# Layer ends, layer starts and gates of a four-block network, reordered on one core

## The chip, the cores and the metric

The kernel runs on one core of a Trainium2 chip. The metric is the device time of one execution in microseconds (us). A core has TensorE (PE, matrix products), VectorE (DVE), ScalarE (ACT), GpSimd (POOL) and SyncE (SP, which here only issues transfers). PEld is TensorE's loading of its stationary operand, PEclk the clock granted to it as a share of full speed. Each engine works through its own instructions in order and meets the others at semaphores.

## The reference

The input x has 256 rows (tokens) of 1024 numbers, all in fp32. Two "first" blocks come first, then a final norm, then two "second" layers of an attention and a feed-forward part each. Cut to what the change touches:

```python
# first block, layer 0 and 1
h = rms_norm(x, norm_w[layer])
(q, k, v, z_attn, q_h, f_h, i_h, g_h, gate_attn, gate_hgrn) = split(h @ w_in[layer])
a = sliding_window_attention(q, k, v, sinks) * silu(z_attn)
o = hgrn2_recurrence(silu(q_h), kin, i_h, logf)       # decays exp(G_t - G_s)
b = rms(o) * hgrn_norm_w * silu(g_h)
merged = sigmoid(gate_attn) * (a @ w_up_attn) + sigmoid(gate_hgrn) * (b @ w_up_hgrn)
x = x + merged @ w_out

# second block, i = 0 and 1; mod comes from silu(c) @ ada_w + ada_b
h = x * (1 + sc_t) + sh_t
y = dsa_mixer(h) if i == 0 else diff_mixer(h)         # each ends in o @ w_o
x = layer_norm(ALPHA * x + (1 + g_t) * y, ln_g[i, 0], ln_b[i, 0])
h = x * (1 + sc_c) + sh_c
y = square(relu(h @ w1)) @ w2                         # 1024 -> 4096 -> 1024
x = layer_norm(ALPHA * x + (1 + g_c) * y, ln_g[i, 1], ln_b[i, 1])
```

## The kernel before

The tokens are two tiles of 128 rows. The stages follow each other: f0 and f1 (the first blocks), s0 (the selecting attention), s1 (feed-forward), s2 (the differential attention) and s3 (feed-forward).

Every product is done in three matmuls, since each fp32 operand is split into a high and a low part: high x high, low x high, high x low (`product_tok`, lines 340 to 342, token-major output, 512 columns at a time; `product_feat`, lines 347 to 349, feature-major output, 256 columns). Weights come in units of 4 k blocks by 512 columns, in halves of 512 KB: SP loads a half into `ring` (line 873), ScalarE casts it to `whi` (line 1037), POOL subtracts that to get `wlo` (line 928), TensorE multiplies. A ring of four units and three slots (PARTS = 3) of `whi`/`wlo` tie these four together. Two more kinds of weights pass through the same ring: the ada_w slabs (line 492), whose products give the modulation of the second layers, and the pieces of s0's latent projection (sixteen small transfers).

What each engine does and when is written out as a program for each. On ScalarE, `ahead(name, more)` casts the weight halves up to three (PARTS) plus `more` beyond those of `name` before the next operation goes; POOL has `lows` for the same. PSUM has eight banks of 512 columns: two turns of two banks for projections (`lin_ps`) and two for everything else (`tmp_ps`). `open_lin` and `open_tmp` on TensorE take the next turn and wait until its last reader has released it.

In the first blocks, the recurrence runs over levels: ScalarE evacuates one projection per level (line 1186: i, z, g, ga0), exps the gate sums (line 1177), VectorE forms factors (lines 1576, 1577) and gathers (line 1586), TensorE multiplies (line 594). Then the attention follows in four groups: scores (line 506), maximum (line 1434), exps (line 1082), transposes (line 402), their copies (line 1097), products (line 529). Between these TensorE runs projections gh0 and gh1; `gate` on ScalarE (line 1199) evacuates ga1, gh0 and gh1 with a sigmoid in the same operation. ACT_TABLE_LOAD stands where ScalarE changes its function table. Then come the transposes bT and aT of the two branches, split by lines 1062 (high) and 1357, 1358 (low), and the products uh0, uh1, ua0, ua1 with `w_up`.

At the end of a layer, `last_by_tiles` runs the last k units of both column halves y0, y1 so that tile 0 is complete first. VectorE's `residual` adds (lines 1759, 1760), takes statistics (lines 1766 to 1768) and, behind POOL's power (line 946), normalises (line 1744; in s3 lines 1750, 1751, which give the result). At the start of the next stage, `turned_by_tiles` transposes x (line 425) into two tmp turns, `keep_busy` (line 408) puts filler matmuls ahead of them (BUSY gives how many), and `mixed` applies the modulation while it splits: ScalarE high (line 1227), VectorE low in pairs of blocks (lines 1716, 1719) and the release of the turn (line 1724). In the feed-forward parts VectorE also scales and shifts x (`affine`, lines 1781, 1784) behind this, and squares the hidden activation (line 1796), which ScalarE casts (line 1257) and VectorE splits (line 1798).

## Time and profile before

| | us |
|---|---|
| median of 3 runs | 1180.23 (1179.15 to 1180.48) |
| profiled execution | 1184.73 |
| its span | 1183.0 |
| PE busy | 1082.4 |
| POOL busy | 772.2 |
| ACT busy | 550.7 |
| DVE busy | 518.8 |

The span is the profiler's stretch from first to last instruction; the profiled execution's own time is 1.7 us more. Busy times of matmuls overlap their neighbours' (they are pipelined), so a stretch of matmuls is best read from the distance of their starts. In a timeline's row, what stands in brackets is the idle time of the engine before it and the instruction that ended it; "DVEq" is VectorE's queue, here the nop at line 1724 that releases a turn. "x8" says that eight such instructions stand in a row.

### The profile page before, as it was taken

The numbers are of one execution on the slowest core, as the hardware profiler recorded it, in microseconds if no ns is written. First come the engines' busy times: TensorE is split into PE (matmuls) and PEld (weight loads), VectorE is DVE, ScalarE is ACT, GpSimd is POOL, SyncE is SP. The second block draws the span as 40 slices with busy tenths as digits, with TensorE's granted clock in tenths as the row PEclk, the third lists the DMA queues.
The fourth block names the chain that finished last, engine by engine and source line by source line (L and its number), as shares of the span: only waits on it lengthen the run. The fifth ranks groups of instructions, "written<-read, shape, count | busy, mean of one in ns | idle before, by whom it ended". The sixth has DMA issues, their size and how long they took to land.

```text
span 1183.0 us, 16461 instructions
## 1 busy us (share of the span) xinstructions
PE 1082.4 (91%) x6654; PEld 911.0 (77%) x6654; DVE 518.8 (44%) x736; ACT 550.7 (47%) x769; POOL 772.2 (65%) x379
## 2 busy tenths in 40 slices
PE   5988989998899999799798999999999698999995
PEld 5776868767778787598576898888888377988984
DVE  5665533336856333347656401114914748110015
ACT  4644555446435564344543444443444434454441
POOL 5785574766946647465025887888786147888884
PEclk9999999999989999999999999999999899999998
DMA  6657542557547335863653867676576723765640
GB/s 241 218 175 274 191 133 96 161 196 228 181 180 280 126 109 160 271 228 90 249 187 116 285 194 240 189 240 194 172 248 228 253 89 107 218 190 180 194 145 36
DMA packets 110786, 221.63 MB, mean 187 GB/s; under 512 B 14721, under 2 KB 21239, under 8 KB 110711
## 3 DMA queue, kind: packets, MB, share of 16 engines
q1 hardware_dynamic: 105536, 210.30, 54.2%
q10 hardware_dynamic: 5174, 10.28, 2.4%
q8 instruction: 53, 0.87, 0.3%
q14 instruction: 23, 0.18, 0.1%
HBM read 219.48 MB, written 1.07 MB: 186 GB/s over the span
## 4 chain that ended last, share of the span: by engine, by line
PE 67%; DVE 14%; POOL 6%; ACT 5%; issue 4%; DMA 3%; SPq 1%; ACTq 0%; DVEq 0%; POOLq 0%
PE lin_ps L340 12%; PE lin_ps L342 11%; PE lin_ps L341 11%; POOL wlo L928 5%; PE tmp_ps L347 4%; PE tmp_ps L349 4%; PE tmp_ps L348 4%; PE lin_ps L347 3%; PE tmp_ps L594 3%; PE lin_ps L349 3%; PE lin_ps L348 3%; PE tmp_ps L492 3%; ACT whi L1037 2%; DMA ring<-in_ada_w 2%; PE tmp_ps L402 1%
## 5 line engine op out<-in xcount | busy, mean ns | idle before, releaser
L928 POOL TENSOR_TENSOR wlo<-ring,whi 128x1024 fp32r<-128x1024 f32 (+2 forms) x304 | 735.1, 2431 | 340.7 <-ACT whi L1037 332.8
L1037 ACT CAST whi<-ring 128x1024 fp32r<-128x1024 f32 (+2 forms) x304 | 313.0, 1034 | 457.0 <-PE lin_ps L342 244.3
L340 PE MATMUL lin_ps<-whi,hThi 128*128 128x512 f32 (+2 forms) x528 | 208.4, 395 | 25.4 <-POOL wlo L928 11.1
L341 PE MATMUL lin_ps<-wlo,hThi 128*128 128x512 f32 (+2 forms) x528 | 202.5, 384 | 0.0
L342 PE MATMUL lin_ps<-whi,hTlo 128*128 128x512 f32 (+2 forms) x528 | 202.4, 383 | 0.0
L347 PE MATMUL tmp_ps<-hThi,whi 128*128 128x256 f32 x520 | 148.0, 285 | 6.8 <-DVEq L1724 5.5
L349 PE MATMUL tmp_ps<-hThi,wlo 128*128 128x256 f32 x520 | 147.4, 283 | 0.0
L348 PE MATMUL tmp_ps<-hTlo,whi 128*128 128x256 f32 x520 | 147.4, 283 | 0.0
L340 PEld LDWEIGHTS lin_ps<-whi,hThi 128*128 128x128 f32 x528 | 100.6, 190 | 59.8 <-issue 18.4
L1796 DVE TENSOR_TENSOR arena<-tmp_ps,arena 128x1024 f32<-128x1024 f32 x16 | 19.6, 1225 | 232.0 <-ACT arena L1252 231.9
L342 PEld LDWEIGHTS lin_ps<-whi,hTlo 128*128 128x128 f32 x528 | 100.5, 190 | 19.9
L341 PEld LDWEIGHTS lin_ps<-wlo,hThi 128*128 128x128 f32 x528 | 100.8, 191 | 17.5
L347 PEld LDWEIGHTS tmp_ps<-hThi,whi 128*128 128x128 f32 x520 | 99.9, 192 | 10.1 <-DVEq L1724 6.4
L347 PE MATMUL lin_ps<-hThi,whi 128*128 128x256 f32 x352 | 100.3, 285 | 5.6 <-DVE hTlo L1352 3.4
L340 PE MATMUL lin_ps<-whi,hbhi 128*128 128x512 f32 x256 | 101.9, 398 | 1.4 <-POOL wlo L928 1.4
L348 PEld LDWEIGHTS tmp_ps<-hTlo,whi 128*128 128x128 f32 x520 | 100.0, 192 | 0.4
L349 PEld LDWEIGHTS tmp_ps<-hThi,wlo 128*128 128x128 f32 x520 | 100.0, 192 | 0.0
L341 PE MATMUL lin_ps<-wlo,hbhi 128*128 128x512 f32 x256 | 99.9, 390 | 0.0
L342 PE MATMUL lin_ps<-whi,hblo 128*128 128x512 f32 x256 | 99.7, 390 | 0.0
L348 PE MATMUL lin_ps<-hTlo,whi 128*128 128x256 f32 x352 | 99.6, 283 | 0.0
L349 PE MATMUL lin_ps<-hThi,wlo 128*128 128x256 f32 x352 | 99.6, 283 | 0.0
L347 PEld LDWEIGHTS lin_ps<-hThi,whi 128*128 128x128 f32 x352 | 67.4, 191 | 7.9 <-POOL wlo L928 3.8
(272 smaller groups left out, 1520.5 us busy)
## 6 DMA issues: line engine op xcount, KB each, us to landing
ring<-in_mlp_w SPq DMA_DIRECT2D x128, 512.0 KB, 4.2
ring<-in_ada_w SPq DMA_DIRECT2D x96, 512.0 KB, 4.7
ring<-in_w_in SPq DMA_DIRECT2D x80, 512.0 KB, 6.1
ring<-in_b_w_in SPq DMA_DIRECT2D x24, 512.0 KB, 4.5
ring<-in_w_out SPq DMA_DIRECT2D x16, 512.0 KB, 3.7
ring<-in_a_w_in SPq DMA_DIRECT2D x12, 512.0 KB, 6.5
ring<-in_w_up_hgrn SPq DMA_DIRECT2D x8, 512.0 KB, 3.8
ring<-in_w_up_attn SPq DMA_DIRECT2D x8, 512.0 KB, 4.0
```

The lines of the kernel that those rows point to most:

```text
L340: pe.matmul(ps, xh, hi, start=first, stop=False, skip_group_check=True)
L341: pe.matmul(ps, xh, lo, start=False, stop=False, skip_group_check=True)
L342: return pe.matmul(ps, xl, hi, start=False, stop=last, skip_group_check=True)
L347: pe.matmul(ps, hi, xh, start=first, stop=False, skip_group_check=True)
L348: pe.matmul(ps, hi, xl, start=False, stop=False, skip_group_check=True)
L349: return pe.matmul(ps, lo, xh, start=False, stop=last, skip_group_check=True)
L402: mm = pe.transpose(ps[:, n * P:(n + 1) * P], piece, ident[:])
L492: mm = pe.matmul(ps[ADA_ROWS * j:ADA_ROWS * (j + 1), 0, :], csil[:, k, :], slot[:, j, :], start=(s == 0), stop=(s == n - 1), skip_group_ch ...
L594: mm = pe.matmul(ps[:, n * P:(n + 1) * P], a, b, start=True, stop=True)
L928: pool.tensor_tensor(wlo[:, n % PARTS, :, 0:width], ring[:, u % RING, 2 * h:2 * h + 2, 0:width], whi[:, n % PARTS, :, 0:width].bitcast(F32 ...
L1037: act.copy(whi[:, n % PARTS, :, 0:width], ring[:, u % RING, 2 * h:2 * h + 2, 0:width]).then_inc(S("high_formed"), 1)
L1796: read(dve.tensor_tensor(h, ps, h, ALU.mult), f"{name}u{g}")
```

## The change

It has four parts.

1. Layer ends (`project`, `mlp`, `last_by_tiles`, `residual`). y0 is completed for both tiles before the last unit(s) of y1; only y1 is done by tiles. VectorE sums both tiles of y0 when it is complete, then tile 0 of y1, normalises tile 0, then tile 1. In `project` the second part of the attention's output is wanted half a unit in. POOL waits for tile 0's x before tile 1's part (`first`).
2. Layer starts (`mixed`, `turned_by_tiles`). Some turns of the transposes are now projection turns (TURNED_IN_LIN), the four blocks of a turn are laid out in the order BANKED, the split goes by single blocks, with each block's own semaphore count for TensorE (`operand(kk)`), and ScalarE waits for VectorE's blocks. The filler counts fall from 8, 8, 16 to 5, 5, 12 in s1, s2, s3; four more stand in the next turn. In s0 the latent pieces are no longer reserved ahead of ada_w.
3. Gates. z, ga0, ga1, gh0 and gh1 are copied out; one Silu and four Sigmoids stand behind the attention. `gate` calls `ahead(name, -PARTS)`. The aT transposes stand in the middle of uh1.
4. Tail. In s3 tile 0's result is formed by VectorE, ScalarE and POOL in turn, tile 1's by VectorE from PSUM; SP waits for each tile's own semaphore.

```diff
 ADA_QUADS = (1, 3, 5, 7)
-BUSY = {"f0": 14, "f1": 4, "s0": 4, "s1": 8, "s2": 8, "s3": 16}
+BANKED = (0, 2, 1, 3)
+TURNED_IN_LIN = {"s0": 1, "s1": 2, "s2": 0, "s3": 2}
...
                     for r, hi, lo in take_halves(HALF, (slice(0, HALF), win(w, c0, HALF, k0))):
-                        operand(k0 + r)
                         for k in range(2):
                             kk = k0 + r + k
+                            operand(kk)
...
+            def last_by_tiles(name, w, pieces):
 
                 held = []
-                for c in range(2):
+                last = {c: n for n, (c, *_) in enumerate(pieces)}
+                for n, (c, k0, src, k_src, first, names) in enumerate(pieces):
+                    ps = opened[f"{name}y{c}"]
                     for r, hi, lo in take_halves(HALF, (slice(0, HALF), win(w, c * HALF, HALF, k0))):
                         operand(k0 + r)
-                        whole = c == 0 and r == 0
+                        ends = n == last[c] and r == 2
+                        whole = n == 0 and r == 0
                         for k in range(2):
                             for i in range(NT if whole else 1):
-                                mm = product_tok(ys[c][:, i, :], src, k_src + r + k, i, hi[:, k, :], lo[:, k, :],
-                                                 False, r + k == 3)
...
+                        if ends:
                             mm.then_inc(S("first_tile"), 1)
                             finished(f"{name}t{c}", (S("first_tile"), bump("first_tile")))
...
+                def turn_a():
+                    pe.wait_ge(S("f_a"), L + 1)
+                    feature_major(f"f{L}aT", hs[:, :, 0:HALF], 4)
...
+                    linear_part(f"f{L}uh{c}", I["w_up_hgrn"][L], c * HALF, HALF, hT, 0, kts=4, k_src=4,
+                                mid=turn_a if c else None)
                 operand_ready(*turned(f"f{L}aT0", 0))
 
...
             def project(name, w):
 
-                def part(c, k0):
-                    linear_part(f"{name}y{c}", w, c * HALF, HALF, hT, k0, half=turn_lin[f"{name}o{c}"][0])
-
                 ada_close()
-                part(0, 0)
-                output_turned(name, 1)
-                part(1, 0)
-                last_by_tiles(name, [opened[f"{name}y{c}"] for c in range(2)], w, 4, hT, 4)
+                linear_part(f"{name}y0", w, 0, HALF, hT, 0, half=turn_lin[f"{name}o0"][0],
+                            mid=lambda: output_turned(name, 1))
+                linear_part(f"{name}y0", w, 0, HALF, hT, 4)
+                opened[f"{name}y1"] = open_lin(f"{name}y1", turn_lin[f"{name}o1"][0])
...
                 for g in range(groups + 1):
                     if g < groups:
-                        feat_units(f"{name}u{g}", open_tmp(f"{name}u{g}"), w1, g * HALF, hT)
+                        ps = open_tmp(f"{name}u{g}")
+                        keep_busy(ps[:, 0, :], 0 if g else 4)
+                        feat_units(f"{name}u{g}", ps, w1, g * HALF, hT)
...
                     if g >= 1:
                         pe.wait_ge(S(f"{name}act"), g)
...
+                        hidden_product(0, g - 1)
+                        if g < groups - 1:
+                            hidden_product(1, g - 1)
+                    if g == groups:
+                        last_by_tiles(name, w2, [(1, 4 * n, (hbhi[:, n % 2], hblo[:, n % 2]), 0, False, (f"{name}hb{n}",))
+                                                 for n in (groups - 2, groups - 1)])
...
-            mixed("s0", lambda: [reserve(*latent(k0)) for k0 in (0, 4)])
+            mixed("s0")
             ps = open_lin("s0misc")
+            keep_busy(ps[:, 0, :], 4)
...
                 for i, after in enumerate((f"{name}t1", f"{name}y1")):
+                    if i and first:
+                        pool.wait_ge(*first)
                     lows(halves_at[after][0] + (1 if i else PARTS), halves_at[after][1])
                     pool.wait_ge(S(f"{name}lnvar"), i + 1)
...
-                        c, dst, func = {2: ("i", vh, ACT.Copy), 4: ("z", zs, ACT.Silu), 6: ("g", zg, ACT.Silu),
-                                        8: ("ga0", ga[:, :, 0:HALF], ACT.Sigmoid)}[lv]
+                        c, dst, func = {2: ("i", vh, ACT.Copy), 4: ("z", zs, ACT.Copy), 6: ("g", zg, ACT.Silu),
+                                        8: ("ga0", ga[:, :, 0:HALF], ACT.Copy)}[lv]
...
                 def gate(name, dst):
-                    ps = full_lin(name)
-                    read(act.activation(dst, ps, ACT.Sigmoid), name)
+                    ahead(name, -PARTS)
+                    ps = full_lin_of(act, name)
+                    read(act.copy(dst, ps), name)
...
                 high_of(f"f{L}bT0", 4, colB[:, 3 + L:4 + L])
+                act.wait_ge(*read_of(f"f{L}gh1"))
+                act.activation(zs[:], zs[:], ACT.Silu).then_inc(S("f_gates"), 1)
+                for c in range(2):
+                    cols = slice(c * HALF, (c + 1) * HALF)
+                    act.activation(gh[:, :, cols], gh[:, :, cols], ACT.Sigmoid).then_inc(S("f_gates"), 1)
+                high_parts(formed[0] + 1, halves_at[f"f{L}aT0"][1])
+                for c in range(2):
+                    cols = slice(c * HALF, (c + 1) * HALF)
+                    act.activation(ga[:, :, cols], ga[:, :, cols], ACT.Sigmoid).then_inc(S("f_gates"), 1)
                 high_of(f"f{L}aT0", 0)
...
             def mixed(name, layer, j):
 
                 for h in range(2):
-                    ps = flat(full_tmp(f"{name}hT{h}"))
+                    ahead(f"{name}hT{h}")
+                    ps = flat(full_turn_of(act, f"{name}hT{h}"))
...
                     for k in range(4):
                         kk = 4 * h + k
-                        ins = act.activation(hThi[:, kk, :], ps[:, k * T:(k + 1) * T], ACT.Identity,
-                                             bias=modc[:, layer, 2 * j, kk:kk + 1],
-                                             scale=modc[:, layer, 2 * j + 1, kk:kk + 1])
-                        if k % 2:
-                            ins.then_inc(S("mixed_high"), 1)
+                        if k >= 2:
+
+                            act.wait_ge(S("mixed_low"), count.get("mixed_act", 0) + kk - 1)
+                        act.activation(hThi[:, kk, :], ps[:, BANKED[k] * T:(BANKED[k] + 1) * T], ACT.Identity,
+                                       bias=modc[:, layer, 2 * j, kk:kk + 1],
+                                       scale=modc[:, layer, 2 * j + 1, kk:kk + 1]).then_inc(S("mixed_high"), 1)
...
-                for k in range(0, KT, 2):
-                    ps = flat(full_tmp_of(dve, f"{name}hT{k // 4}"))[:, (k % 4) * T:(k % 4 + 2) * T]
+                for k in range(KT):
+                    turn = f"{name}hT{k // 4}"
+                    ps = flat(full_turn_of(dve, turn))[:, BANKED[k % 4] * T:(BANKED[k % 4] + 1) * T]
                     dve.wait_ge(S("mixed_high"), bump("mixed_whole"))
-                    for h in range(2):
-                        v = ps[:, h * T:(h + 1) * T]
-                        ins = dve.tensor_scalar(v, v, modc[:, layer, 2 * j + 1, k + h:k + h + 1],
-                                                modc[:, layer, 2 * j, k + h:k + h + 1], ALU.mult, ALU.add)
-                    step(ins)
-                    ins = dve.tensor_tensor(flat(hTlo[:, k:k + 2, :]), ps, flat(hThi[:, k:k + 2, :].bitcast(F32)),
-                                            ALU.subtract)
-                    ins.then_inc(S("mixed_low"), 1)
-                    if k % 4:
-                        dve.wait_ge(S("mixed_low"), bump("mixed_done", 2))
-                        dve.nop().then_inc(read_of(f"{name}hT{k // 4}")[0], 1)
+                    step(dve.tensor_scalar(ps, ps, modc[:, layer, 2 * j + 1, k:k + 1], modc[:, layer, 2 * j, k:k + 1],
+                                           ALU.mult, ALU.add))
+                    dve.tensor_tensor(hTlo[:, k, :], ps, hThi[:, k, :].bitcast(F32), ALU.subtract
+                                      ).then_inc(S("mixed_low"), 1)
+                    if k % 4 == 3:
+                        dve.wait_ge(S("mixed_low"), bump("mixed_done", 4))
+                        dve.nop().then_inc(read_of(turn)[0], 1)
...
-                for i in range(NT):
-                    normalised(i)
+
+                dve.wait_ge(*done[f"{name}y0"])
+                summed(0, 0)
+                summed(1, 0)
+                dve.wait_ge(*done[f"{name}t1"])
+                summed(0, 1)
+                statistics(0)
+                if n < 3:
+                    normalised(0)
+                else:
+                    dve.wait_ge(S("lnp_landed"), 32 * (n + 2))
+                    for c in range(2):
+                        cols = slice(c * HALF, (c + 1) * HALF)
+                        dve.scalar_tensor_tensor(x[:, 0, cols], x[:, 0, cols], mv[:, 0, 0:1], lnp[:, 0, cols],
+                                                 ALU.subtract, ALU.mult).then_inc(S("centred"), 1)
+                dve.wait_ge(*done[f"{name}y1"])
+                summed(1, 1)
+                statistics(1)
+                if n < 3:
+                    normalised(1)
+                else:
...
+                    for c in range(2):
+                        cols = slice(c * HALF, (c + 1) * HALF)
+                        ps = lin_ps[:, 2 * turn_lin[f"{name}y{c}"][0] + 1, :]
+                        ins = dve.scalar_tensor_tensor(ps, ps, mv[:, 1, 0:1], lnp[:, 0, cols], ALU.subtract, ALU.mult)
+                    step(ins)
+                    dve.wait_ge(S(f"{name}lnrstd"), 2)
+                    for c in range(2):
+                        cols = slice(c * HALF, (c + 1) * HALF)
+                        ps = lin_ps[:, 2 * turn_lin[f"{name}y{c}"][0] + 1, :]
+                        dve.scalar_tensor_tensor(x[:, 1, cols], ps, st[:, 2, 1, 0:1], lnp[:, 1, cols], ALU.mult, ALU.add
+                                                 ).then_inc(S("result1"), 1)
```

ScalarE around the gates of layer 0, before, up to the first copy of transposed scores (whi is a weight cast; line 1199 evacuates ga1 and then gh0; line 1082 are the attention's exps):

```order
L1196 ACTIVATE hs<-lin_ps 128x2x512
L1037 CAST whi<-ring 128x1024 x2
L1199 ACTIVATE arena<-lin_ps 128x2x512
L1082 ACT_TABLE_LOAD
L1082 ACTIVATE arena,qst<-arena,qst 128x128 x4
L1107 ACTIVATE qst<-qst 128x4
L1082 ACTIVATE arena,qst<-arena,qst 128x128 x4
L1107 ACTIVATE qst<-qst 128x4
L1037 CAST whi<-ring 128x1024 x4
L1199 ACT_TABLE_LOAD
L1199 ACTIVATE arena<-lin_ps 128x2x512
L1097 COPY arena<-tmp_ps 128x512
```

The same after the change (line 1083 is the cast, line 1246 the evacuation, line 1128 the exps):

```order
L1242 ACTIVATE hs<-lin_ps 128x2x512
L1246 COPY arena<-lin_ps 128x2x512
L1128 ACTIVATE arena,qst<-arena,qst 128x128 x4
L1153 ACTIVATE qst<-qst 128x4
L1083 CAST whi<-ring 128x1024 x2
L1128 ACTIVATE arena,qst<-arena,qst 128x128 x4
L1153 ACTIVATE qst<-qst 128x4
L1083 CAST whi<-ring 128x1024
L1246 COPY arena<-lin_ps 128x2x512
L1083 CAST whi<-ring 128x1024 x3
L1143 COPY arena<-tmp_ps 128x512
```

The two casts that stood ahead of ga1's evacuation stand behind the first four exps; of the four behind the second group one still stands ahead of gh0's evacuation and three behind it; both table loads are gone.

SP at the start of s0, before, the last of the latent's sixteen pieces (in_a_w_in_2) and what follows:

```order
L873 DMA ring<-in_a_w_in 128x2x256
L873 DMA ring<-in_a_w_in 128x2x8
L873 DMA ring<-in_a_w_in 128x2x64 x2
L873 DMA ring<-in_ada_w 128x1024 x4
L873 DMA ring<-in_a_w_in 128x2x512 x12
```

SP after the change, from the last transfers of f1 on:

```order
L910 DMA ring<-in_w_out 128x2x512 x4
L910 DMA ring<-in_ada_w 128x1024 x4
L910 DMA ring<-in_a_w_in 128x2x256
L910 DMA ring<-in_a_w_in 128x2x8
L910 DMA ring<-in_a_w_in 128x2x64 x2
```

The four ada_w transfers moved from behind the sixteen pieces to ahead of them.

VectorE at the end of s0, from the sums of tile 1 to the first blocks of s1 (x is the residual, gmod the gate, mv and st the statistics), before:

```order
L1759 TENSOR_TENSOR lin_ps<-lin_ps,gmod 128x512
L1760 SCALAR_TENSOR_TENSOR x<-x,lin_ps 128x512
L1766 BN_STATS bns<-x 128x6
L1759 TENSOR_TENSOR lin_ps<-lin_ps,gmod 128x512
L1760 SCALAR_TENSOR_TENSOR x<-x,lin_ps 128x512
L1766 BN_STATS bns<-x 128x6
L1767 BN_AGGR mv<-bns 128x2
L1768 TENSOR_SCALAR mv<-mv 128x1
L1744 TENSOR_SCALAR x<-x,mv,st 128x1024 x2
L1406 COPY adaacc<-tmp_ps 128x512
L1716 TENSOR_SCALAR tmp_ps<-tmp_ps,modc 128x256 x2
L1719 TENSOR_TENSOR hTlo<-tmp_ps,hThi 128x512
```

The same place after the change:

```order
L1823 BN_AGGR mv<-bns 128x2
L1824 TENSOR_SCALAR mv<-mv 128x1
L1804 TENSOR_SCALAR x<-x,mv,st 128x1024
L1812 TENSOR_TENSOR lin_ps<-lin_ps,gmod 128x512
L1813 SCALAR_TENSOR_TENSOR x<-x,lin_ps 128x512
L1819 BN_STATS bns<-x 128x6
L1823 BN_AGGR mv<-bns 128x2
L1824 TENSOR_SCALAR mv<-mv 128x1
L1804 TENSOR_SCALAR x<-x,mv,st 128x1024
L1470 COPY adaacc<-tmp_ps 128x512
L1779 TENSOR_SCALAR lin_ps<-lin_ps,modc 128x256
L1781 TENSOR_TENSOR hTlo<-lin_ps,hThi 128x256
```

Of tile 1 only the second column is summed behind tile 0's statistics; the first has moved ahead. Tile 0 is normalised before that sum, and the split goes by one block of 256 columns in a projection's turn instead of by two.

## Rows read from the trace of the kernel before

**Rows 1.** The page: busy time by engine, and the chain's shares.

```profile
PE 1082.4 (91%) x6654; PEld 911.0 (77%) x6654; DVE 518.8 (44%) x736; ACT 550.7 (47%) x769; POOL 772.2 (65%) x379
...
PE 67%; DVE 14%; POOL 6%; ACT 5%; issue 4%; DMA 3%; SPq 1%; ACTq 0%; DVEq 0%; POOLq 0%
```

**Rows 2.** Waits: engine, line waited for; us in total, times, longest.

```profile
PE tmp_ps L347 <- DVEq L1724: 5.5, 2, 2.8
...
PE lin_ps L340 <- ACT arena L1199: 7.0, 4, 2.0
```

**Rows 3.** Timeline (start us, us, engine, line, what), layer 0, level 5.

```profile
105.16 1.28 ACT L1186 ACT_TABLE_LOAD   x1
...
116.67 1.59 PE L594 MATMUL tmp_ps<-arena 128*128 128x128 f32 x7 [3.36 <-DVE arena L1586]
```

**Rows 4.** Windows (stretch, length, busy PE, PEld, DVE, ACT, POOL; PEclk; DMA); timeline.

```profile
84.00:90.00 6.00, 5.05 (x24) 3.89 (x28) 3.26 (x5) 0.00 (x0) 0.25 (x1) 0.53 0.01 3
116.00:121.00 5.00, 4.33 (x20) 4.14 (x21) 1.96 (x4) 1.02 (x1) 2.36 (x1) 0.66 0.67 249
176.90:182.00 5.10, 5.04 (x15) 3.98 (x16) 1.28 (x6) 4.59 (x13) 0.42 (x1) 0.67 0.51 182
414.00:420.00 6.00, 4.54 (x20) 3.77 (x21) 2.63 (x8) 5.96 (x14) 1.85 (x1) 1.00 0.56 186
...
84.95 3.75 PE L594 MATMUL tmp_ps<-arena 128*128 128x128 f32 x16 [4.85 <-DVE arena L1577]
```

**Rows 5.** Timeline of ScalarE, POOL, TensorE around the gates, layer 0.

```profile
156.46 1.05 ACT L1037 CAST whi<-ring 128x1024 fp32r<-128x1024 f32 x1 [2.64 <-PE lin_ps L342]
...
159.18 1.05 ACT L1037 CAST whi<-ring 128x1024 fp32r<-128x1024 f32 x1 [1.67 <-PE lin_ps L342]
160.13 1.02 ACT L1199 ACTIVATE arena<-lin_ps 128x1024 f32<-128x1024 f32 x1
...
163.31 0.40 ACT L1082 ACTIVATE arena<-arena,qst 128x128 f32<-128x128 f32 x1 [0.86 <-DVE qst L1434]
...
158.26 4.72 POOL L928 TENSOR_TENSOR wlo<-ring,whi 128x1024 fp32r<-128x1024 f32 x2
...
173.05 0.39 PE L342 MATMUL lin_ps<-whi,hTlo 128*128 128x512 f32 x1
...
176.97 0.50 PE L340 MATMUL lin_ps<-whi,hThi 128*128 128x512 f32 x1 [2.02 <-ACT arena L1199]
...
182.35 0.39 PE L341 MATMUL lin_ps<-wlo,hThi 128*128 128x512 f32 x1
182.58 0.39 PE L342 MATMUL lin_ps<-whi,hTlo 128*128 128x512 f32 x1
```

**Rows 6.** Timeline of TensorE behind the transposes of a, layer 0.

```profile
213.57 0.46 PE L340 MATMUL lin_ps<-whi,hThi 128*128 128x512 f32 x1 [1.69 <-DVE hTlo L1357]
```

**Rows 7.** Timeline of the DMA queue and TensorE at the start of s0.

```profile
475.64 8.62 SPq L873 DMA_DIRECT2D ring<-in_a_w_in  x16
...
492.89 1.93 PE L492 MATMUL tmp_ps<-ring,csil 128*32 128x512 f32 x8 [1.45 <-DMA ring<-in_ada_w]
...
502.02 0.36 PE L340 MATMUL lin_ps<-whi,hThi 128*128 128x264 f32 x1 [2.90 <-DVEq L1724]
```

**Rows 8.** Timeline of TensorE and VectorE in s1, and in s2's projection.

```profile
644.27 0.39 PE L347 MATMUL tmp_ps<-hThi,whi 128*128 128x256 f32 x1 [2.69 <-DVEq L1724]
...
652.59 6.67 DVE L1784 TENSOR_TENSOR x<-x,lnp 128x1024 f32<-128x1024 f32 x2
...
665.53 0.39 PE L347 MATMUL tmp_ps<-hThi,whi 128*128 128x256 f32 x1 [0.82 <-POOL wlo L928]
...
956.04 1.29 DVE L1926 TENSOR_TENSOR hs<-lin_ps,st 128x512 f32<-128x512 f32 x2 [1.76 <-POOL st L939]
```

**Rows 9.** Timeline of TensorE and VectorE at the end.

```profile
1171.08 0.39 PE L342 MATMUL lin_ps<-whi,hblo 128*128 128x512 f32 x1
...
1179.82 0.75 DVE L1751 SCALAR_TENSOR_TENSOR x<-x,st,lnp 128x512 f32<-128x512 f32 x1
```

164 lines of the change are left out of this document (92 added, 72 removed).

## The prediction

> **What bounds the kernel now.** I read the page first. TensorE is busy 91% of the span and holds 67% of the chain that ended last; VectorE has 14%, POOL 6%, ScalarE 5% [rows 1]. TensorE's arithmetic is the same in both kernels, so the change can only win what TensorE waits for (and its clock), and can only lose by making it wait anew. The view of waits says what those waits are: at the gates 7.0 us for ScalarE's evacuations in 4 times, at the starts of the two feed-forward layers 5.5 us for VectorE's release of a PSUM turn [rows 2]. The rest comes from timelines around four places: the last level of the recurrence [rows 3], the gates and the attention beside them [rows 5, 6], the start of s0 [rows 7], and the end of the kernel [rows 9]. None is a single large stall, so it is a sum of small terms, and one new stall of 5 us is enough to undo several.
>
> TensorE's clock has to be carried along. In two stretches of the recurrence, behind gaps of 4.85 and 3.36 us, the granted clock was 0.53 and 0.66, behind the gate's 2.02 us gap 0.67 in layer 0, but 1.00 behind its like in layer 1 [rows 3 to 5]. At full clock projection matmuls start 0.23 us apart [rows 5], so a half unit of 12 takes 2.73 us, and at 0.53 it takes 5.1. A gap near 2 us thus costs itself and sometimes more: 5.04 busy us at 0.67 are 1.6 us too many [rows 4].
>
> **The change part by part.** The sum is made against the profiled execution (1184.73 us, span 1183.0).
>
> A, recurrence, layer 0. The output gate z is now copied, so its table load and the one like it before the level's exp go: 2 x 1.28 us [rows 3]. Behind them the chain exp, factors, gather ends in TensorE's 3.36 us wait, followed by a low clock: 4.33 busy us at 0.66 are 1.5 us too many [rows 4]. VectorE cannot start all of the 2.57 us earlier if POOL shares its time, so: the loads alone give -2.6, stall and clock all together -5.0; I take -4.5, near the upper end since the whole wait hangs on ScalarE's exp. In layer 1 no such stall stands, 0. The Trainium skill (page "ScalarE: Activation LUTs", section "What ACT_TABLE_LOAD costs") says that a load is followed by a drain, about 2.66 us a switch together; by that the two would give 5.3 us, and A could reach its upper end by ScalarE alone. The trace does not bear it out: the operation after the load at 105.16 starts 20 ns after its end [rows 3].
>
> B, gates, both layers. Five table loads around the attention go (1.28 us each) and ga0, ga1, gh0, gh1 become copies; two loads and five activations come behind the attention. But `gate` now stops the weight casts at the unit being evacuated, and the first exps of the attention stand before the next two casts. In the trace those casts ran at 156.46 and 159.18 [rows 5], before the evacuation at 160.13 and before the exps, which wait for VectorE's maximum until 163.31, whatever ScalarE does before. After the change: exps and normaliser end at about 165.0, casts to 166.1 and 167.1, and POOL's split of 2.4 us each (4.72 us for two) [rows 5] gives TensorE its next half at 168.65. TensorE has one half ready (160.2 to 162.95) and then idles 5.7 us. gh0, which ended at 173.44, ends at 176.85; the three casts behind its evacuation then let gh1 stall about 3.0 us, and it ends at 186.9 instead of 184.33. Against this the transposes of a move into the middle of a unit: the 1.69 us wait for hTlo [rows 6] and some 0.35 of its neighbour go. Without the clock: layer 0 +0.6, layer 1 +2.1 (there no 1.6 us of low clock is won back). With it: behind 5.7 us half clock is near certain, +2.4 per layer (a half unit at 5.1 less 2.73); behind 3.0 us it comes in about six cases of ten at 1.5, so +0.9. Together +9.3; bounds +2.7 (no low clock) and +12 (all of it).
>
> C, start of s0. SP issued the 16 small latent transfers first, 8.62 us, and then four ada_w transfers; TensorE waits for ada_w (1.45 us at 492.89, and about as long once before it), then 2.90 us for VectorE's release before 502.02 [rows 7]. Now ada_w goes first and the transposes lie in a projection bank, so the 3.0 us and the 2.9 us go, and the first block can be multiplied when it alone is split: the latent product starts near 495.9 instead of 502.0. I take -6.2; bounds -5.0 (latent pieces landing late take 1.2 back) and -7.5. The later ada slabs lose nothing, since the ring stays four units deep.
>
> D, starts of s1, s2, s3. The 2.69 us wait [rows 8] and its like at s3 fall by about 1.9 by the blocks and the earlier first column. Most is given back: VectorE's affine on x behind the split is long (its second pair 6.67 us, slowed by POOL beside it), and it is this which sets the hidden activation, ScalarE's casts behind that and POOL's split, on which TensorE waits at 665.53 [rows 8]. VectorE's own start moves only 0.9 earlier. So -0.8 each for s1 and s3 (bounds 0 and -1.9), s2, which has no such affine, -1.2 (-0.9 to -1.7). Sum -2.8, bounds -0.9 and -5.5.
>
> E, new waits. In the projection of s2 the second part of the operand is now wanted half a unit in; VectorE delivers it only after the operation at 956.04 (two of 0.64, ends 957.33) [rows 8], +0.7. In the feed-forward ends the activation of the last group is asked for before the first column's product, +0.35 each. Queued behind the waiting instruction on TensorE are its products alone, and nobody else waits for those. Sum +1.4, bounds 0 and +2.5.
>
> F, end. Before, VectorE still had both columns of tile 1 ahead of it when TensorE was nearly done (its last product starts at 1171.08), then for each tile and column two operations of 0.75, up to 1180.57 [rows 9]; the span ends 2.4 us later. Now one column of tile 1 is done ahead, tile 0's second half of the work is ScalarE's and POOL's, and of tile 1 there remain, at the same 0.75 an operation, three for the column, 0.2 for the statistics, two beside POOL's power and two behind it: 5.5 us after 1171.5, so 1177.0, 3.6 earlier. I take -2.9, since tile 0's results stand ahead in SP's queue; bounds -2.0 and -3.6.
>
> Sum: -4.5 + 9.3 - 6.2 - 2.8 + 1.4 - 2.9 = -5.7 us, so 1184.73 becomes 1179.0. The profiled execution lies 4.5 us above the median of the runs (1180.23); the forecast for the median is 1174.5.
>
> **The rivals.**
> 1, the gates gain what they seem to. If the attention's maximum comes earlier than 163, because ScalarE no longer loads tables, or the two casts slip in ahead, TensorE never starves: the gaps of 2.02 with 1.6 of clock, 1.69 and 0.35 go in layer 0 (-5.7), 2.03, 1.69 and 0.35 in layer 1 (-4.1). Then the sum is -24.8: 1155.4. Against it: the maximum's operations follow the scores of 159.0 on VectorE, not ScalarE.
> 2, it starves but the clock holds: B is +2.7, the sum -12.3: 1167.9. For it: layer 1's gap without a fall of the clock; against it: its length was 2 us, not 5.7.
> 3, slower: the clock falls at every place where TensorE is left idle or has less to do. There are the two new gaps in each layer (B without any luck: 4.6 + 6.1 = +10.7) and the starts of s1 and s3, where 8 filler matmuls become 5 and 16 become 12 and the wait stays above 0.8 us (+1.5 each). With A at -2.6, C -5.0, D -2.2, E +1.4 and F -2.5 that is +2.8: 1183. It decides from about +9 us of clock price on. For it: 0.67 behind 2.02 us; against it: full clock behind the waits of s1 and s3 as they are.
> 4, no change: the earlier starts at s0 to s3 are given back wholly, since POOL's 65% busy time makes its split the pace of the next units (C at -2, D at 0), and B at +9.3: sum -0.7 to 0, 1180.
>
> **How the numbers follow.** Chances: forecast 0.52, rival 1 0.10, rival 2 0.14, rival 3 0.13, rival 4 0.11. The forecast's own range is 1168 to 1180 (A to F at their bounds, added as independent, about 6 us). The range over all reaches rival 2, half of the way to rival 1 and almost rival 3: 1161 to 1182. Faster by over 0.2% (2.4 us, what a measurement of this kernel can tell) is rivals 1 and 2 and nine tenths of the forecast, 0.71; within it 0.15 (rival 4 and the forecast's edge); slower 0.14.
>
> **What would show it.** A: no wait at L594 in front of the last level of layer 0. B: TensorE idle about 5.7 us behind the first half of gh0 with POOL's split as the releaser, and a granted clock near 0.5 behind it; two casts between the exps of the attention and none before. C: the latent product starts some 6 us earlier relative to f1's end, no ada_w wait. D: shorter first waits in s1 and s3 but a longer wait for POOL in the last half of the second unit. F: 7.8 us from the last product to the end instead of 11.5. I am wrong if the gates show no gap above 3 us, or the stages after their starts show the early time kept.

## The result, and the profile after

| | before | changed |
|---|---|---|
| median of 7 runs, us | 1181.07 (1179.15 to 1186.0) | 1186.9 (1185.81 to 1193.82) |
| ratio, 95% interval | | 1.0065 (1.0045 to 1.0086) |
| span of the profiled run, us | 1183.0 | 1192.1 |

The changed kernel is slower, by 0.65%, some 7.7 us. The forecast was 1174.5 in a range of 1161 to 1182. A second set of five runs gave 1.0071 (1.0059 to 1.0084).

The page of the changed kernel, busy time and the chain's shares (against [rows 1]):

```profile
PE 1089.9 (91%) x6644; PEld 916.7 (77%) x6644; DVE 533.0 (45%) x750; ACT 548.9 (46%) x771; POOL 773.0 (65%) x381
...
PE 72%; DVE 12%; POOL 6%; issue 4%; ACT 4%; DMA 2%; ACTq 0%; DVEq 0%; POOLq 0%
```

TensorE is busy 7.5 us more though its arithmetic is the same; its mean granted clock is 0.971 where it was 0.978. Its waits have changed names. In the view of waits (line waited for; us in total, times, longest) the entries of [rows 2] are down to 0.9 us or gone, and POOL's split (line 965) has come in their place:

```profile
PE lin_ps L342 <- POOL wlo L965: 29.5, 15, 5.0
...
PE tmp_ps L349 <- POOL wlo L965: 8.9, 6, 4.1
...
PE lin_ps L342 <- ACT arena L1246: 0.9, 2, 0.5
...
ACT hbhi L1316 <- DVE arena L1882: 33.3, 16, 7.1
```

Both kernels run the same 4968 product matmuls, so the n-th of one can be set against the n-th of the other. The table gives us between the starts of two of them (the last column: from the last product's start to the end of the span):

```
kernel              level 5  gates 0  gates 1  s0 start  s1 start  s2 start  s3 start  tail
before                 32.0     57.4     58.7      61.8      52.7      33.6      48.0  11.92
changed                31.4     61.2     64.6      57.9      54.8      33.3      50.1   8.72
changed, again         27.9     61.0     65.0      57.7      54.9      33.3      50.2   8.67
e1 gate casts          30.5     51.9     54.8      56.6      55.8      33.3      49.3   8.72
e2 affine spread       31.4     61.2     65.0      57.6      47.9      33.3      43.6   8.70
e3 act pairs           31.4     61.0     64.8      54.8      53.7      32.0      47.8   8.69
e5 all                 26.7     51.9     54.8      54.8      48.1      32.0      43.8   8.70
e7 before, ada first   28.8     57.3     58.9      58.7      53.1      33.6      49.9  11.92
e8 all, old ends       31.4     51.9     54.7      54.8      50.2      34.9      45.9  10.71
e10 ga1 casts          26.8     57.0     58.8      57.7      56.3      33.3      49.8   8.70
```

Outside the first column, kernels that share a stage's code agree within 1.6 us; s3's start of the kernel before is an exception (48.0 here, 49.9 in e7 and again in e11). There the clock differs: behind the same wait TensorE was granted 1.00 in the kernel before and 0.50, the lower of its two levels (1.2 and 2.4 GHz), in e7. First the kernel before, then e7:

```profile
988.77 0.38 PE L347 MATMUL tmp_ps<-hThi,whi 128*128 128x256 f32 x1 [2.83 <-DVEq L1724]
...
988.70:994.70 6.00, 5.93 (x49) 1.00 0.32 106
```

```profile
979.51 0.58 PE L347 MATMUL tmp_ps<-hThi,whi 128*128 128x256 f32 x1 [2.85 <-DVEq L1724]
...
979.50:985.50 6.00, 5.99 (x28) 0.50 0.40 105
```

The table shows both halves of the result: s0's start and the tail gained 3.9 and 3.2 us, the gates lost 3.8 and 5.9 us, s1's start 2.1 us and s3's as much (but only 0.2 against e7's). The columns account for 5.9 of the 9.1 us between the two spans; the other 3.2 us lie in the stretches between them, which in the second profile of the changed kernel are 1.0 us longer than before.

TensorE in layer 0's gates after the change (start us, us), against [rows 5]:

```profile
160.87 0.50 PE L342 MATMUL lin_ps<-whi,hThi 128*128 128x512 f32 x1 [0.46 <-ACT arena L1246]
...
168.93 0.80 PE L342 MATMUL lin_ps<-whi,hThi 128*128 128x512 f32 x1 [5.05 <-POOL wlo L965]
...
184.08 0.76 PE L342 MATMUL lin_ps<-whi,hThi 128*128 128x512 f32 x1 [3.07 <-POOL wlo L965]
```

Windows of TensorE (stretch, length, busy, PEclk, DMA share and GB/s) behind its new gaps, two in each layer's gates and the one in s1:

```profile
168.90:174.00 5.10, 5.07 (x13) 0.55 0.62 195
184.00:188.40 4.40, 4.32 (x13) 0.64 0.58 166
410.40:416.00 5.60, 5.52 (x13) 0.52 0.57 190
426.00:430.50 4.50, 4.49 (x13) 0.62 0.55 178
672.20:676.50 4.30, 4.24 (x24) 0.65 0.87 262
```

The cause stands in ScalarE's and POOL's timeline of the same stretch:

```profile
159.80 1.01 ACT L1246 COPY arena<-lin_ps 128x1024 f32<-128x1024 f32 x1 [5.31 <-PE lin_ps L344]
163.78 0.40 ACT L1128 ACTIVATE arena<-arena,qst 128x128 f32<-128x128 f32 x1 [2.96 <-DVE qst L1498]
...
165.43 1.97 ACT L1083 CAST whi<-ring 128x1024 fp32r<-128x1024 f32 x2
...
166.53 4.68 POOL L965 TENSOR_TENSOR wlo<-ring,whi 128x1024 fp32r<-128x1024 f32 x2 [7.57 <-ACT whi L1083]
...
179.54 1.01 ACT L1246 COPY arena<-lin_ps 128x1024 f32<-128x1024 f32 x1 [9.56 <-PE lin_ps L344]
180.45 2.94 ACT L1083 CAST whi<-ring 128x1024 fp32r<-128x1024 f32 x3
```

ScalarE was idle for 5.31 us, then for 2.96 and 9.56 us, each time at the head of its queue with ready casts behind it. In the kernel before, casts at 156.46 and 159.18 stood in the first of these idle times.

The start of s0 and the end, TensorE and VectorE (against [rows 7] and [rows 9]):

```profile
505.77 0.36 PE L342 MATMUL lin_ps<-whi,hThi 128*128 128x264 f32 x1
...
1183.38 0.39 PE L344 MATMUL lin_ps<-whi,hblo 128*128 128x512 f32 x1
...
1187.76 1.41 DVE L1856 SCALAR_TENSOR_TENSOR x<-lin_ps,st,lnp 128x512 f32<-128x512 f32 x2
```

The latent's first product no longer waits at all, and VectorE is done 5.4 us after TensorE's last product ends, where it took 9.1 us before.

### The profile page after: what moved, and what is told of

It is laid out like the page before. It is cut to its first block, busy times and chain, and to the rows that moved or that the text cites. A ratio compares the mean times of both kernels' runs of the same rounds, so it can differ in the third digit from the quotient of the medians.

```text
span 1192.1 us, 16479 instructions
## 1 busy us (share of the span) xinstructions
PE 1089.9 (91%) x6644; PEld 916.7 (77%) x6644; DVE 533.0 (45%) x750; ACT 548.9 (46%) x771; POOL 773.0 (65%) x381
## 4 chain that ended last, share of the span: by engine, by line
PE 72%; DVE 12%; POOL 6%; issue 4%; ACT 4%; DMA 2%; ACTq 0%; DVEq 0%; POOLq 0%
PE lin_ps L342 13%; PE lin_ps L343 13%; PE lin_ps L344 13%; POOL wlo L965 5%; PE tmp_ps L349 4%; PE tmp_ps L351 4%; PE tmp_ps L350 4%; PE tmp_ps L616 3%; PE lin_ps L349 3%; PE lin_ps L350 3%; PE lin_ps L351 3%; PE tmp_ps L514 2%; PE tmp_ps L404 2%; PE lin_ps L551 2%; ACT whi L1083 2%
## 5 line engine op out<-in xcount | busy, mean ns | idle before, releaser
L342 PE MATMUL lin_ps<-whi,hThi 128*128 128x512 f32 (+2 forms) x528 | 211.5, 401 | 29.7 <-POOL wlo L965 27.6
L343 PE MATMUL lin_ps<-wlo,hThi 128*128 128x512 f32 (+2 forms) x528 | 205.4, 389 | 0.0
L344 PE MATMUL lin_ps<-whi,hTlo 128*128 128x512 f32 (+2 forms) x528 | 204.9, 388 | 0.0
```

The costliest lines, as they stand in the source:

```text
L342: pe.matmul(ps, xh, hi, start=first, stop=False, skip_group_check=True)
L343: pe.matmul(ps, xh, lo, start=False, stop=False, skip_group_check=True)
L344: return pe.matmul(ps, xl, hi, start=False, stop=last, skip_group_check=True)
```

## Experiments

All ratios are against the kernel before, with 95% intervals; the changed kernel stands at 1.0065, or 1.0071.

**e1, casts ahead at the gates.**

```diff
                 def gate(name, dst):
-                    ahead(name, -PARTS)
+                    ahead(name)
```

> The changed kernel with one number undone: `gate` lets the weight casts run three halves beyond the unit it evacuates, as before the change, while the gates stay copies with the sigmoids behind the attention. Theory (the casts' place in ScalarE's queue starves TensorE): the waits for POOL of 5.05 and 3.07 us at gh0 and gh1 in each layer and the half clock behind them go. They cost 3.85 and 5.9 us net of what the copies and the earlier transposes of a gain; without them each layer's gates gain some 4 us instead. So about -18 us against the changed kernel, 0.985 to 0.99 of it, faster than the kernel before (about 1170). Rival (the copies or the late sigmoids themselves delay the chain): TensorE still waits 3 us or more at the same two places, only for the evacuation or the exps, and the time stays within 4 us of the changed kernel.

Measured: 0.9912 (0.9895 to 0.9929), median 1171.02: 1.5% and 18 us below the changed kernel. Both POOL waits at the gates are gone (gates 61.2 and 64.6 become 51.9 and 54.8 us) and what is left in layer 0 are three short waits. The theory holds, the rival falls.

```profile
158.71 0.50 PE L342 MATMUL lin_ps<-whi,hThi 128*128 128x512 f32 x1 [1.46 <-ACT arena L1246]
...
167.89 0.50 PE L342 MATMUL lin_ps<-whi,hThi 128*128 128x512 f32 x1 [0.72 <-POOL wlo L965]
...
173.01 0.50 PE L342 MATMUL lin_ps<-whi,hThi 128*128 128x512 f32 x1 [0.60 <-ACT arena L1246]
```

**e10, casts ahead at ga1 only.**

```diff
-                def gate(name, dst):
-                    ahead(name, -PARTS)
+                def gate(name, dst, more=-PARTS):
+                    ahead(name, more)
...
-                          {0: lambda: gate(f"f{L}ga1", ga[:, :, HALF:D]),
+                          {0: lambda: gate(f"f{L}ga1", ga[:, :, HALF:D], 0),
```

> The changed kernel with the casts restored at one of the three evacuations only, ga1's, which stands ahead of the attention's first exps. Theory (each stall has its own queue place): the 5.05 us wait at gh0 and the low clock behind it go in both layers, the 3.07 us wait behind gh0's evacuation stays or shrinks by less than half; two thirds of the 18 us, -11 to -13 against the changed kernel, about 0.996. Rival (the second stall is only the first one's echo): both go, and the time is that of the full repair, 0.991.

Measured: 0.9972 (0.9959 to 0.9985), 11.7 us below the changed kernel by the second set. The wait of 5.05 is gone, the other stands unchanged:

```profile
172.36 0.77 PE L342 MATMUL lin_ps<-whi,hThi 128*128 128x512 f32 x1 [3.08 <-POOL wlo L965]
```

Two places in ScalarE's queue, two prices: the stage table gives 4.2 and 5.8 us per layer for the first and 5.1 and 4.0 us for the second, low clock included.

**e11, the gates' part alone on the kernel before, with `ahead(name)`.**

```diff
-                    ps = full_lin(name)
-                    read(act.activation(dst, ps, ACT.Sigmoid), name)
+                    ahead(name)
+                    ps = full_lin_of(act, name)
+                    read(act.copy(dst, ps), name)
```

(and z, ga0, the late silu and sigmoids and `turn_a` as in the change)

> The kernel before with the gates' part alone (copies, late silu and sigmoids, transposes of a in the middle of uh1), the weight casts running ahead as before. Theory (the part is worth what the forecast's first rival said, if ScalarE's queue does not starve TensorE): the 2.02 us waits at gh1, the 1.69 us waits behind the transposes of a and some low clock go, -8 to -10 us, 0.992. Rival (the late sigmoids stand on the path): -4 us or less.

Measured: 0.992 (0.9905 to 0.9934), median 1170.72. The idea of the part is worth 10 us; one number in it cost 18.

**e2, the scale and shift of x out of the way.**

```diff
-                affine(n - 1, name)
                 for g in range(8):
...
+                    if g < 4:
+                        affine_part(n - 1, name, g)
```

(`affine_part` is one of its four operations; `norm_weights` moves from group 1 to group 5)

> The changed kernel with VectorE's scale and shift of x in s1 and s3 taken out of the way: its four operations stand one each behind the first four hidden groups, and ScalarE's loading of the next norm weights stands at group 5 instead of 1. Theory (the earlier start of s1 and s3, 4.06 and 4.04 us, is given back because the 13 us of that scale and shift now hold up the square, ScalarE's queue behind it and so POOL's split): the waits of 4.11 and 3.74 us in the second unit of s1 and s3 and the half clock behind each go, -4 to -5 us per layer, -8 to -10 in all. Rival (POOL's pace beside VectorE is the bound: 3.1 us a half where TensorE needs 2.88): TensorE waits for POOL just as long, spread over more halves, -3 us or less.

Measured: 0.9982 (0.997 to 0.9993), 0.83% and 9.8 us below the changed kernel; s1's start 54.8 to 47.9, s3's 50.1 to 43.6. Of these 13.4 us some 3 are given back later in the same stages: behind their starts the rest of s1 took 162.1 us instead of 160.5, that of s3 162.3 instead of 160.6; why, no run shows. How the start was given back shows in the changed kernel's s1, VectorE and ScalarE, then TensorE (against [rows 8]):

```profile
652.99 6.37 DVE L1867 TENSOR_TENSOR x<-x,lnp 128x1024 f32<-128x1024 f32 x2 [0.24 <-DVE hTlo L1781]
659.39 6.65 DVE L1870 TENSOR_TENSOR x<-x,lnp 128x1024 f32<-128x1024 f32 x2
666.07 1.22 DVE L1882 TENSOR_TENSOR arena<-tmp_ps,arena 128x1024 f32<-128x1024 f32 x1
...
667.33 1.05 ACT L1316 CAST hbhi<-arena 128x1024 fp32r<-128x1024 f32 x1 [7.14 <-DVE arena L1882]
...
668.74 1.04 ACT L1083 CAST whi<-ring 128x1024 fp32r<-128x1024 f32 x1 [0.36 <-issue]
...
672.26 0.58 PE L349 MATMUL tmp_ps<-hThi,whi 128*128 128x256 f32 x1 [4.11 <-POOL wlo L965]
```

TensorE began the stage's first products 4 us sooner, but VectorE's 13 us of affine ended no sooner in the stage than before (44.3 us after its start, against 43.4), and the cast of hbhi at the head of ScalarE's queue held the weight casts 7.14 us: TensorE had gained 4.06 us, waited 4.11 us, and went on at a clock of 0.65. In the kernel before, the same cast waited 2.5 us at most. In e2 hbhi waits 1.4 us at most:

```profile
ACT hbhi L1316 <- DVE arena L1895: 22.0, 16, 1.4
...
PE tmp_ps L349 <- POOL wlo L965: 1.9, 5, 0.4
```

**e3, blocks in pairs, ScalarE free.**

```diff
-BANKED = (0, 2, 1, 3)
+BANKED = (0, 1, 2, 3)
...
-                        if k >= 2:
-                            act.wait_ge(S("mixed_low"), count.get("mixed_act", 0) + kk - 1)
...
-                    dve.wait_ge(S("mixed_high"), bump("mixed_whole"))
+                    if k % 2 == 0:
+                        dve.wait_ge(S("mixed_high"), bump("mixed_whole", 2))
```

> The changed kernel with ScalarE's waits in `mixed` taken away: the blocks lie in the natural order and VectorE starts on a pair of blocks when ScalarE has done both, while TensorE still takes single blocks. Theory (ScalarE, held by VectorE's blocks, casts late): in s0 the 1.84 us wait for POOL in the latent product goes with its low clock, -2 to -3 us, against 0.5 us later first blocks at each of four starts; sum -1 to +1. Rival (the latent's wait comes from its casts being wanted earlier, whatever ScalarE waits for): the wait stays, and the sum is +1 to +2.

Measured: 1.0012 (1.0 to 1.0024), 6 us below the changed kernel, more than either theory said. In s0 the change went as the theory has it: 57.9 to 54.8 us. But the other starts gained too (s1 1.1, s2 1.3, s3 2.4 us). At each of them the first cast behind the blocks comes 1.6 us sooner in the stage, and POOL's split with it, so that the affine's first operation runs in 1.22 us where it took 3.02 beside the split. The long waits for POOL in s1 and s3 stand (3.98 and 3.61 us). VectorE in e3's s1, against 652.99 above:

```profile
648.69 4.57 DVE L1865 TENSOR_TENSOR x<-x,lnp 128x1024 f32<-128x1024 f32 x2 [0.24 <-DVE hTlo L1779]
```

The edit changes the order of the blocks and their pairing as well as ScalarE's waits, and no run parts the three. ScalarE and TensorE in s0 of the changed kernel:

```profile
509.64 0.56 ACT L1287 ACTIVATE hThi<-tmp_ps,modc 128x256 fp32r<-128x256 f32 x1 [1.59 <-DVE hTlo L1781]
510.56 0.56 ACT L1287 ACTIVATE hThi<-tmp_ps,modc 128x256 fp32r<-128x256 f32 x1 [0.35 <-DVE hTlo L1781]
...
511.50 2.74 ACT L1083 CAST whi<-ring 128x784 fp32r<-128x784 f32 x3 [0.38 <-issue]
...
514.33 0.39 PE L342 MATMUL lin_ps<-whi,hThi 128*128 128x264 f32 x1 [1.84 <-POOL wlo L965]
```

**e7, the kernel before with ada_w ahead of the latent.**

```diff
-            mixed("s0", lambda: [reserve(*latent(k0)) for k0 in (0, 4)])
+            mixed("s0", lambda: None)
```

> The kernel before, with one thing changed: the latent's sixteen transfers are no longer reserved ahead of the four of ada_w at the start of s0. Theory (the ada_w waits of 1.55 and 1.45 us go, but the transposes' wait for their bank and for the split stays): -2 to -3 us. Rival (SP's order is the whole gain of s0's start): -5 us or more; or (the latent's pieces now land late) no gain, with a wait for the ring or POOL of 2 us or more in the latent product.

Measured: 0.9977 (0.9962 to 0.9991), -2.7 us; s0's start 61.8 to 58.7. The wait for the split stands, as the theory said:

```profile
493.73 0.36 PE L340 MATMUL lin_ps<-whi,hThi 128*128 128x264 f32 x1 [2.73 <-DVEq L1724]
```

**e4, z by its silu again.**

```diff
-4: ("z", zs, ACT.Copy)
+4: ("z", zs, ACT.Silu)
...
-                act.activation(zs[:], zs[:], ACT.Silu)
+                act.activation(zs[:], zs[:], ACT.Copy)
```

> The changed kernel with z evacuated by the silu again in the fourth level (and a plain copy where its silu stood behind the attention), so two table loads of 1.28 us stand again ahead of the fifth level's exp and one behind the attention goes. Theory (those loads were hidden: without them VectorE's differences and factors run beside POOL's split at 2.9 us each instead of 0.7 to 0.8): no change, within 2 us. Rival (as forecast): the loads are on the path, +3 to +5 us.

Measured: 1.0093 (1.0073 to 1.0113) from six runs of 1187.15 to 1195.62. That is 3 us above the changed kernel, but the intervals overlap, and in its profile the stretch took 28.3 us, less than the changed kernel's 31.4. By itself this run decides nothing. The profiles side by side say more. Up to level 5 the changed kernel (twice), e1, e2, e3, e5, e6, e8 and e10 are the same program, and their stretch of 84 products took 26.7 to 31.4 us (the kernel before and e7, the same program there too: 32.0 and 28.8). Two things go together with its length: how many of VectorE's four operations of that level ran beside POOL's split (some 2.9 us each instead of 0.7), and whether the table loads stand there.

```
profile                table loads   slowed   TensorE's wait   PEclk   level 5
before                 yes           2        3.36 (VectorE)   0.95    32.0
e7                     yes           1        1.57 (VectorE)   1.00    28.8
e4                     yes           1        1.36 (VectorE)   1.00    28.3
changed, e2, e3, e8    no            3        2.85 (VectorE)   0.95    31.4
changed, again         no            2        0.91 (VectorE)   1.00    27.9
e5, e10                no            1        none             1.00    26.7, 26.8
e6, e11                no            0        0.89, 0.72 (POOL) 1.00   27.9, 27.7
e1                     no            0        1.92 (POOL)      0.94    30.5
```

At the same number of slowed operations the stretch is 1.5 to 4.1 us shorter without the loads, so they were on the path, against this run's theory. But without them VectorE also starts sooner, and in four of the nine profiles three operations instead of two ran beside the split. And where none did, TensorE waited for the split instead. This is read from single profiles; no run fixes the number of slowed operations and changes the loads alone. First the changed kernel, then e1 (VectorE, POOL, TensorE):

```profile
107.64 2.88 DVE L1620 TENSOR_TENSOR arena<-arena 128x512 f32<-128x512 f32 x1
110.44 2.90 DVE L1640 TENSOR_TENSOR arena<-arena 128x512 f32<-128x512 f32 x1
...
107.09 5.69 POOL L965 TENSOR_TENSOR wlo<-ring,whi 128x1024 fp32r<-128x1024 f32 x2
...
117.37 2.03 PE L616 MATMUL tmp_ps<-arena 128*128 128x128 f32 x14 [2.85 <-DVE arena L1650]
```

```profile
106.85 0.69 DVE L1640 TENSOR_TENSOR arena<-arena 128x512 f32<-128x512 f32 x1 [0.44 <-ACT arena L1223]
107.46 0.85 DVE L1641 TENSOR_TENSOR arena<-arena 128x512 f32<-128x512 f32 x1
...
109.08 7.02 POOL L965 TENSOR_TENSOR wlo<-ring,whi 128x1024 fp32r<-128x1024 f32 x3
...
111.50 0.75 PE L342 MATMUL lin_ps<-whi,hThi 128*128 128x512 f32 x1 [1.92 <-POOL wlo L965]
```

**e9, POOL held back there, on e5.**

```diff
                 ins.then_inc(S("f_rope"), 1)
+                if L == 0:
+                    pool.wait_ge(S("level_ready"), 6)
```

> The kernel of all three repairs, with POOL held back once, in layer 0 before its splits beside the fifth level, until VectorE has formed that level's factors. Up to there the changed kernel and five experiments are the same program, and yet the level went in two ways: three operations of VectorE at 2.85 to 2.90 us beside POOL's split, or all at 0.69 to 0.85 us with POOL idle. Theory (it is chance which comes first, and worth some 5 us): held back, the fast way comes every time, -1 to -3 us in the median against the kernel of all repairs. Rival (POOL's split is wanted at once): TensorE waits 2 us or more for it and the median stays or grows.

Measured: 0.9792 (0.9779 to 0.9806), against 0.9774 (0.975 to 0.9798) for e5: no gain. In its profile all of VectorE's operations there took 0.69 us and TensorE did not wait, as the theory has it. The stretch took 27.3 us, but 26.7 in e5's profile without the hold. That the hold helps is not shown.

**e12, the changed kernel again.**

> The changed kernel itself once more, beside these on the same chip. Theory: 1.005 to 1.009 of the kernel before, with its executions some 6 us apart by the outcome of the fifth level of layer 0; the profile shows VectorE's operations there either at 0.7 to 0.85 or at 2.85 us. Rival: all executions alike, within 2 us.

Measured: 1.0071, five runs within 1188.27 to 1190.22. The rival's "all alike" is what came; in the first set seven runs fell into 1185.8 to 1186.9 and 1192.0 to 1193.8. So the stretch varies between sets as well, and its share in the spread was not settled. In this profile two operations were slowed, and the stretch took 27.9 us.

**e5, all three repairs; e6, the same with the old tail; e8, the same with the old layer ends.**

```diff
 # e8, in project; mlp and residual alike
-                linear_part(f"{name}y0", w, 0, HALF, hT, 4)
-                opened[f"{name}y1"] = open_lin(f"{name}y1", turn_lin[f"{name}o1"][0])
-                last_by_tiles(name, w, [(1, 0, hT, 0, True, ()), (1, 4, hT, 4, False, ())])
+                linear_part(f"{name}y1", w, HALF, HALF, hT, 0, half=turn_lin[f"{name}o1"][0])
+                last_by_tiles(name, w, [(0, 4, hT, 4, False, ()), (1, 4, hT, 4, False, ())])
```

> The changed kernel with all three repairs together: weight casts ahead at the gates, VectorE's scale and shift of x spread over the first four hidden groups, and blocks split in pairs without ScalarE's waits. Theory (three separate places where an instruction waits at the head of an in-order queue and keeps POOL's split late): the three gains add up, since they lie at the gates, at the feed-forward starts and mostly at s0: 0.9912, 0.9982 and 1.0012 against 1.0065 are -18, -10 and -6 us, so some 1152 to 1157, 0.976 to 0.980 of the kernel before. Rival (they share one bound, POOL's pace of splits): no more than the best two, 1160 or above.

> The kernel of all three repairs, with the end of s3 as before the change: both tiles normalised by VectorE in x behind both statistics, no ScalarE or POOL part. Theory (the tail saves 2.9 to 3.6 us, since nothing stands behind it that could give it back): +3 us against the kernel of all repairs, the stretch from TensorE's last product to the end 11 us instead of about 8. Rival (the early sums of the first column are the saving, not the tail): within 1 us.

> The kernel of all three repairs, with the ends of s0 to s3 as before: the last k unit of both column halves by tiles, VectorE summing tile by tile (tile 0 still normalised ahead of tile 1's sums). Theory (VectorE's two sums moved ahead of the last unit shorten each stage's start by about 2 us when nothing downstream gives it back): +5 to +8 us over the four ends. Rival (TensorE's wait at a stage start is set by the split of the blocks, not by the sums): within 2 us.

Measured: e5 0.9774 (0.975 to 0.9798), median 1155.18, 26 us faster than the kernel before, the best version; in the total the three gains add up (18, 10 and 6 us, 34 below the changed kernel). At s1 and s3 what e3 gained does not come on top of e2 (48.1 and 43.8 us against 47.9 and 43.6), and level 5 had its shortest outcome in this profile. e6 0.9802 (0.9779 to 0.9825), tail 11.30 us instead of 8.70: the tail is worth its 3 us, from the profile; the times alone barely part the two. e8 0.9862 (0.9836 to 0.9887), 10 us above e5. Of that the table shows 2.1, 2.9 and 2.1 us at the starts of s1, s2 and s3 and 2.0 in the tail, 9 together; its profile, of the slowest of its six runs, also had the long level 5. The early first column pays, once nothing behind it gives it back.

## Why the prediction was wrong

The sign was wrong: -5.7 us forecast, +7.7 measured, and +9.1 between the two profiled spans. Step by step, in the spans:

- **B, gates, right.** +9.3 forecast with gaps of 5.7 and 3.0 us; measured +3.8 and +5.9, together +9.7, with gaps of 5.05 and 3.07 and a clock of 0.52 to 0.64 behind all four. Rival 1, which gave these stages -9.8 us, was worth doing as a repair: e11.
- **A, level 5 of layer 0, wrong in what the wait hung on.** The forecast let the whole 3.36 us wait hang on ScalarE's exp. The loads did go and the exp began sooner, but the wait only fell to 2.85, since three of VectorE's operations ran beside POOL's split (2.88 us each, or 0.69 alone) where it had been two. -4.5 forecast, -0.6 in this profile, -4.1 in the second one of the same kernel. What the term is worth on average stays open.
- **C, s0, half right.** ada_w first gave its 3 us (e7). The rest came at the first block: up to the fourth piece of the latent TensorE was 7.5 us ahead, the upper bound of the term. In that piece 3.6 us were given back, the 1.84 us wait and a clock of 0.64 behind it: ScalarE, made to wait for VectorE's blocks, cast it late. -6.2 forecast, -3.9 measured; without these waits (e3) -7.1. That ScalarE's new waits stand ahead of weight casts was not in the sum; the forecast asked what is queued behind a wait for TensorE's waits only.
- **D, s1 to s3, wrong in sign, and the largest miss.** The forecast said that "most is given back" and named the affine, the cast of hbhi and POOL's split, but let a remainder of 0.8 us stand in each of s1 and s3 from a sum of two differences. Measured at the starts: s1 +2.1, s2 -0.3, s3 +2.1 (+0.2 against e7's s3). The gain came to nothing or less because the affine now ran beside POOL throughout (13.0 us, against 4.57 + 6.67 before), the cast of hbhi held the weight casts 7.1 us, and each new 4 us wait brought 1.3 to 1.5 us of low clock, which the forecast kept for a rival. For s2 the forecast says that no affine stands there. One does, from 853.45 on for 13 us, and TensorE waits for POOL 0.15 to 0.30 us four times beside it.
- **E**, +1.4 forecast: the first unit of s2's projection took 0.8 us more, and the two feed-forward ends have a new wait of 0.32 us each. **F**, -2.9 forecast, -3.2 measured. Both right.

Forecast and spans lie 14.8 us apart. D has 6.7 of them, A 3.9 and C 2.3; B and F nearly cancel, and the rest lies between the stages. So the step that failed is the same in D and C: time won at a start was booked as kept, without the wait at the head of ScalarE's queue that would hold POOL's next split.

Of the rivals the third, slower, came, at +7.7 instead of +2.8. Half of its reason came with it: new gaps at the gates with a low clock behind them (+10.7 there, +9.7 measured). At the starts of s1 and s3, where it expected the low clock from fewer filler matmuls, the clock was 1.00 (643.60 to 650.00 and 992.00 to 1000.00); it fell only behind the waits for POOL in the second unit. It was given 0.13, and its price was too low because it had A and C as gains larger than came, by 2.0 and 1.1 us, and D, clock included, at +0.8 where +3.9 came. The fourth rival's terms (C at -2, D at 0, B at +9.3) give +1.3 with A, E and F as forecast, not the -0.7 to 0 that it states; that would have been 1181.5.

Of its two signs of being wrong neither came: the gates have gaps above 3 us, and s1 and s3 do not keep the early time. In D the forecast named the chain that takes it back and had its size wrong.

## What to carry to other kernels

When one in-order engine feeds the rest (ScalarE's casts, then POOL's split, then TensorE), each instruction moved in its queue must be followed by asking which casts now stand behind it and for how long it waits. Here waits in three places of that queue's way (the gates, the blocks' split, the cast of hbhi) part a kernel 26 us faster than the one before from one 7.7 us slower. The affine ahead of the square stood in the kernel before too, and spreading it was not tried there, so how much of the 26 us is the change's own is open. A stage that starts earlier keeps the time only if the slowest chain inside it (here 13 us of scale and shift that nothing needed yet) starts earlier too or is moved out. And a stall whose releaser ran beside another engine's long operation can come out differently in the next execution: look at several profiles before booking it as a gain.

## What the runs showed of the hardware

A VectorE operation of two 128x512 fp32 inputs took 0.69 us alone and 2.85 to 2.90 us beside POOL's split of 128x1024, four times as long; a 128x1024 one of the affine took 1.2 us alone and 3.0 to 3.4 beside it. The split itself took 2.4 us alone, 2.8 to 2.9 beside the smaller operations and 3.1 to 3.4 beside the affine. This is a race: in nine profiles of the same instructions zero to three of VectorE's operations were slowed.

The granted clock, a mean of its two levels (0.5 and 1) over a window, fell to 0.52 to 0.65 behind the five new gaps of 3.07 to 5.05 us whose windows are shown. Behind shorter gaps the length alone did not decide it: behind the 1.84 to 1.86 us wait in s0 it was 0.64 in both profiles of the changed kernel and 1.00 in e1; behind 2.0 us at the gates it fell once of twice [rows 4]; behind 2.83 to 2.85 us in s3 it stayed at 1.00 in the kernel before and was 0.50 in e7. After 3.36 us [rows 3] and 4.85 us [rows 4] it had fallen too.
